# Block-wise products in the three merges of the triangular inverse

## The reference, cut to what matters

```
a = where(strict, einsum('bhnid,bhnjd->bhnij', k_beta, k) * decay, 0.0)
rhs = concatenate([v * beta, k_beta * exp(cum)])
sol = triangular_solve(a + eye, rhs, lower=True, unit_diagonal=True)
```

## Time and profile before

| | |
|---|---|
| median of 3 runs | 2837.27 us (2835.69 to 2837.76) |
| profiled execution | 2833.87 us |
| its span, first to last instruction | 2832.0 us |
| mean granted TensorE clock | 0.930 |
| PE / DVE / ACT / POOL busy | 91% / 51% / 28% / 7% |
| passes at L938, L948, L927 | 480, 480, 160 |

### The profile page before, as it was taken

The page is one execution under the profiler, slowest core; times in us unless marked ns, Lnnn a source line. Parts: engine busy times, 40 slices in busy tenths (PEclk is TensorE's granted clock), DMA queues, the critical chain, the costliest instruction groups (busy, mean ns, idle before and its releaser), DMA issues.

```text
span 2832.0 us, 39867 instructions
## 1 busy us (share of the span) xinstructions
PE 2587.9 (91%) x16152; PEld 2269.9 (80%) x16152; DVE 1454.4 (51%) x2004; ACT 801.6 (28%) x1031; POOL 204.1 (7%) x166
## 2 busy tenths in 40 slices
PE   6998888868899999998998899999898778999998
PEld 6997888857799999998987688887685444688886
DVE  5776555655345344453364567667414555434433
ACT  5322222212422212231222322223222354323222
POOL 1000101011000000010000100002001200100001
PEclk9997999989699999999976999999898889899998
DMA  3222222231122222222200254444221000122221
GB/s 125 87 75 71 78 78 74 59 86 31 76 78 88 90 90 89 89 99 81 76 13 0 89 178 165 152 158 163 97 74 45 0 0 0 61 103 89 96 97 60
DMA packets 91921, 230.90 MB, mean 82 GB/s; under 512 B 59946, under 2 KB 61564, under 8 KB 67620
## 3 DMA queue, kind: packets, MB, share of 16 engines
q1 hardware_dynamic: 86272, 197.04, 21.6%
q10 hardware_dynamic: 5540, 32.30, 3.3%
HBM read 217.67 MB, written 11.64 MB: 81 GB/s over the span
## 4 chain that ended last, share of the span: by engine, by line
PE 78%; DVE 11%; DMA 4%; ACT 3%; issue 2%; POOL 0%; DVEq 0%; SPq 0%; ACTq 0%; POOLq 0%
PE ps L285 60%; DMA g_D<-scr_g 2%; PE ps L449 2%; PE ps L475 1%; PE ps L948 1%; PE ps L938 1%; PE ps L289 1%; DVE wlo L308 1%; PE ps L2122 1%; PE ps L2104 1%; DVE g_tmp L1082 1%; PE ps L1571 1%; PE ps L1572 1%; PE ps L955 1%; DVE a_mx L2188 1%
## 5 line engine op out<-in xcount | busy, mean ns | idle before, releaser
L285 PE MATMUL ps<-xa_hi,whi 128*128 128x264 f32 (+1 forms) x2512 | 656.4, 320 | 44.0 <-DVE wlo L308 19.8
L285 PE MATMUL ps<-xa_lo,whi 128*128 128x264 f32 (+1 forms) x2512 | 652.1, 319 | 0.0
L285 PE MATMUL ps<-xa_hi,wlo 128*128 128x264 f32 (+1 forms) x2512 | 649.8, 318 | 0.0
L308 DVE TENSOR_TENSOR wlo<-raw,whi 128x2048 fp32r<-128x2048 f32 x161 | 373.5, 2320 | 261.2 <-ACT whi L301 261.2
L285 PEld LDWEIGHTS ps<-xa_hi,whi 128*128 128x128 f32 x2512 | 419.2, 191 | 86.6 <-issue 33.2
L301 ACT ACTIVATE whi<-raw 128x2048 fp32r<-128x2048 f32 x161 | 307.5, 1910 | 598.0 <-PE ps L285 581.1
L285 PEld LDWEIGHTS ps<-xa_lo,whi 128*128 128x128 f32 x2512 | 419.4, 191 | 29.7
L285 PEld LDWEIGHTS ps<-xa_hi,wlo 128*128 128x128 f32 x2512 | 418.6, 191 | 30.3
L285 PE MATMUL ps<-xb_hi,whi 128*128 128x264 f32 (+1 forms) x1280 | 384.0, 340 | 9.9 <-DVE xb_lo L1688 8.1
L285 PE MATMUL ps<-xb_lo,whi 128*128 128x264 f32 (+1 forms) x1280 | 385.1, 341 | 0.0
L285 PE MATMUL ps<-xb_hi,wlo 128*128 128x264 f32 (+1 forms) x1280 | 383.6, 340 | 0.0
(11 more groups left out here) (386 smaller groups left out, 2919.8 us busy)
## 6 DMA issues: line engine op xcount, KB each, us to landing
raw<-weights SPq DMA_DIRECT2D x161, 1024.0 KB, 4.9
mod_w<-weights_mod ACTq DMA_DIRECT2D x24, 1024.0 KB, 4.8
g_EC<-scr_g SPq DMA_DIRECT2D x10, 424.0 KB, 4.8
scr_z<-z_st SPq DMA_DIRECT2D x16, 264.0 KB, 2.4
g_D<-scr_g SPq DMA_DIRECT2D x10, 371.0 KB, 6.2
scr_a<-g_AT SPq DMA_DIRECT2D x10, 318.0 KB
h<-x_in ACTq DMA_DIRECT2D x4, 528.0 KB, 8.2
z_a<-scr_z SPq DMA_DIRECT2D x1, 2112.0 KB, 12.4
```

Of the source, the lines that this page charges most:

```text
L285: mm = pe.matmul(ps[:, at_ + step * c + bank, 0:tn], w[:, hb.slot, k, c * P:(c + 1) * P], x[:, k, t0:t0 + tn], start=(k == 0 and n == 0), ...
L308: dve.tensor_tensor(wlo[:, hb.slot], raw[:, hb.raw_slot], whi[:, hb.slot].bitcast(F32), ALU.subtract).then_inc(S("w_lo"), 1)
```

## The change

The products of a merge are cut to the blocks that it needs. A new function lists them: three pairs in merge 0 (32x32 tiles at 0, 32, 64, of which the products use 16 columns), two in merge 1 (32 wide, the second with 10 rows), one in merge 2 (64 by 42). The transposes become products with the identity on the same tiles. As some columns of the PSUM banks are then never written by these products, DVE clears columns 264 to 511 of banks 0 to 2 and 4 to 6 at the head of the stage, in place of a mere increment of the semaphore `z_ev`, and PE waits for both before its first product.

```diff
--- before.py
+++ after.py
@@ -846,6 +846,14 @@
 
             return slice(t // 2 * CH, t // 2 * CH + CH)
 
+        def tiles_of_merge(l):
+
+            if l == 0:
+                return [(slice(a, a + 2 * BLK), slice(a, a + 2 * BLK), a, a + BLK, BLK, BLK) for a in range(0, 6 * BLK, 2 * BLK)]
+            n = 2 * BLK * l
+            return [(slice(a, a + n), slice(a + n, min(CH, a + 2 * n)), a, a + n, n, min(CH, a + 2 * n) - a - n) for a in range(0, CH, 2 * n)
+                    if a + n < CH]
+
         def groups_of(t):
 
             return [(x, 2 * (t % 2) + x) for x in range(2)]
@@ -924,7 +932,8 @@
                             if l == 1 and z < N_Z:
                                 pe.wait_ge(S("z_ev"), 2 + nth(z, x))
                             for q in range(4):
-                                mm = pe.transpose(ps[0:CH, 4 * x + 1, q * CH:(q + 1) * CH], g_U[0:CH, 4 * x + q, 0:CH], ident[0:CH, 0:CH])
+                                for a, _, i, _, n, _ in tiles_of_merge(l):
+                                    mm = pe.matmul(ps[a, 4 * x + 1, q * CH + i:q * CH + i + n], g_U[a, 4 * x + q, a], ident[a, a], start=True, stop=True)
                             mm.then_inc(S("g_uT"), 1)
                     for x, g in groups_of(t):
                         if l:
@@ -935,8 +944,9 @@
                             if t < HALVES - 1:
                                 pe.wait_ge(S("g_A"), nth(t + 1, x))
                         for q in range(4):
-                            mm = pe.matmul(ps[0:CH, 4 * x, q * CH:(q + 1) * CH], g_AT[t % 2][0:CH, 4 * x + q, :], g_TV[0:CH, 4 * x + q, 0:CH],
-                                           start=True, stop=True)
+                            for a, b, i, _, n, _ in tiles_of_merge(l):
+                                mm = pe.matmul(ps[b, 4 * x, q * CH + i:q * CH + i + n], g_AT[t % 2][a, 4 * x + q, b], g_TV[a, 4 * x + q, i:i + n],
+                                               start=True, stop=True)
                         mm.then_inc(S("g_P"), 1)
                     for x, g in groups_of(t):
                         pe.wait_ge(S("g_Pc"), 2 * MERGES * t + 2 * l + x + 1)
@@ -945,8 +955,9 @@
                             if z < N_Z:
                                 pe.wait_ge(S("z_ev"), 2 + nth(z, x))
                         for q in range(4):
-                            mm = pe.matmul(ps[0:CH, 4 * x + 2, q * CH:(q + 1) * CH], g_B1[0:CH, 4 * x + q, :], g_U[0:CH, 4 * x + q, 0:CH],
-                                           start=True, stop=True)
+                            for a, b, i, j, n, m in tiles_of_merge(l):
+                                mm = pe.matmul(ps[i:i + n, 4 * x + 2, q * CH + j:q * CH + j + m], g_B1[b, 4 * x + q, i:i + n], g_U[b, 4 * x + q, j:j + m],
+                                               start=True, stop=True)
                         mm.then_inc(S("g_XU"), 1)
                 for x, g in groups_of(t):
                     pe.wait_ge(S("g_r"), nth(t, x))
@@ -970,6 +981,7 @@
                                        start=True, stop=True)
                     mm.then_inc(S("g_inc"), 1)
 
+            pe.wait_ge(S("z_ev"), 2)
             kk(0)
             for n in range(Z_EARLY):
                 z_block(n)
@@ -1149,7 +1161,8 @@
                 if z < N_Z:
                     dve_split(dve, HalfBlock(HB_GDN_OUT + z + 2))
 
-            dve.sem_inc(S("z_ev"), 2)
+            for x in range(2):
+                dve.memset(ps[:, 4 * x:4 * x + 3, 2 * P + 8:4 * P], 0.0).then_inc(S("z_ev"), 1)
             dve.wait_ge(S("in"), IN_FIRST + 32)
             differences(0)
             matrices(0)
```

## The result

The changed kernel takes 2845.82 us, the median of 8 runs (2841.41 to 2848.49), against 2835.90 us for the kernel before, also 8 runs (2832.46 to 2837.82). The ratio is 1.0035, with a 95% interval of 1.0024 to 1.0045: +9.9 us, slower. The forecast was 2861, +23.6. The profiled execution of the changed kernel took 2848.49 us (span 2846.6), 14.6 us more than the profiled one of before (2833.87), so the two traces have somewhat more to explain than the medians do.

The account below looks back on a forecast made before the run. PE and the merges' PE-ACT-DVE ring were taken to bind almost equally. Steps +15.8, low-clock excess -13.5 and +1.6 give +3.9; with clock +18 and clearing +1.7, +23.6 us: 2857 profiled, median 2861, range 2820 to 2893.

Parts of the forecast that it names:

- rival (d): Small passes step at 53 ns and the clock stays as now: +5.6 us, 2843; chance 0.18.
- I take the middle, 53 ns: Step between PE passes up to 32 wide in the merges, taken between 31 and 76 ns.
- +15.8: Merges over ten halves at full clock: us added by 2400 passes instead of 1120, at 53 or 58 ns each.
- the lower bound: PE step scaled down with operand width: 31 ns for 32 wide, 58 ns for 64 wide.
- rival (b): Merge tiles on different rows and columns run side by side: ring -18.4, excess -8, clearing +1.7; -25 us, 2812; chance 0.10.
- Small passes hardly feel the clock: Merges at the lower clock: a small pass takes 58 ns against 53 at full clock.
- the ring: Each merge's cycle: PE transpose, ACT copy, PE product P, ACT copy, PE product XU, DVE predicated copy; 4.52 us in merge 1.
- low-clock excess: Extra time of merge 0 and 1 groups running at the lower clock before; expected to go, -13.5 us.
- +1.6: Merges: us left at the lower clock, some 300 small passes at 5 ns each.
- nothing to give, as said: Merge 2 gains nothing in nine halves, as DVE's small inverses for the next half cover it; -0.45 us in the last.
- The clock term: Clock still low at L955 behind the merges: 3.6 instead of 1.79 us per half, +18 us; ends 0 and about +35.
- The clearing: Two PSUM memsets at the stage head delay the first product: +1.7 us on the chain, between +0.5 and +2.3.

Follow-up runs that it names:

- Experiment 4: Kernel before with the PSUM clearing and only merge 2 cut to its 64 by 42 tile: 2861.61 us, ratio 1.0099.
- experiment 3: Kernel before with the PSUM clearing and merges 0 and 1 in tiles, merge 2 over the full 106: 2837.20 us, ratio 1.0008.
- experiments 8: Kernel before, no tiles or clearing, with unused wide products (10, 24 and 4) filling PE's large idle gaps: 2828.24 us, ratio 0.9992.
- 10: Changed kernel with PE's large gaps and the handovers in every merge filled by unused products of dense data: 2874.84 us, ratio 1.0146.
- experiment 1: Kernel before with only the two PSUM memsets and PE's wait for them: 2834.43 us, ratio 0.9999.
- experiments 2: Kernel before with the PSUM clearing and only merge 0 in 32x32 tiles: 2842.82 us, ratio 1.0031.
- experiment 12: Kernel before with the PSUM clearing, only merge 0 tiled, and PE's large gaps filled by unused products of dense data: 2842.83 us, ratio 1.0026.
- experiments 5: Changed kernel with unused wide products filling PE's large idle gaps around merge 0: 2840.82 us, ratio 1.0030.
- 13: Kernel before with the clearing; in merge 2 alone P and XU use 64 and 42 rows, all 106 columns: 2847.64 us, ratio 1.0050.

## Why the prediction was right or wrong, step by step

**Direction and mechanism held, the size didn't.** Slower by over 0.2% had the largest chance. The time lies in the range, but 15 us under the forecast, and nearest to rival (d), which gets its 2843 from a clock that stays as it was: right number, wrong reason.

**The failed step is "I take the middle, 53 ns", the term of the sum that gave +15.8.** The step is 10.7 ns on three tiles, about 15 ns on two ((0.33 - 0.11) / 15 at 706.03). It has two parts. On one tile a pass of 32 columns takes 32 ns and one of 64 columns 58 ns: that is the lower bound which I had carried down in proportion to the width (31 and 58 ns), and the reason to go above it, "two instructions for each pass must cost something that doesn't shrink", was wrong. And the tiles run beside each other, rival (b)'s mechanism, to which I gave 0.10. The earlier trace rows were the wrong neighbour for that: they load 88 columns on all 128 rows. "Small passes hardly feel the clock" fell too: the same 48 passes at granted clock 0.50 take 1.05 us (t = 8), a step of about 19 ns.

**Rival (b)'s gain came only in part.** It had -18 for the ring and -8 of excess, and the merges give -14.3. By half: the four z halves t = 0, 1, 3, 4 give -14.5, the other six together +0.3. Cut at the predicated copies of x = 0, us before and after:

| halves | first P to copy of merge 0 | from there to copy of merge 1 | from there to L955 / L966 |
|---|---|---|---|
| t = 0 to 5 | 29.0, 32.8 | 40.2, 23.3 | 36.7, 36.1 |
| t = 6 to 8 | 13.6, 7.0 | 14.0, 19.7 | 17.9, 18.0 |
| t = 9 | 3.8, 4.0 | 4.5, 3.7 | 5.3, 6.0 |

In the z halves the gain is in the middle column. Its lines in t = 1, DVE of the kernel before and of the changed one:

```profile
373.27 0.62 DVE L1135 COPY_PREDICATED g_U<-g_maskU,ps 106x424 f32<-106x424 uint32 x1
...
380.58 0.65 DVE L1135 COPY_PREDICATED g_U<-g_maskU,ps 106x424 f32<-106x424 uint32 x1 [2.50 <-PE ps L948]
```

```profile
375.64 1.32 DVE L1147 COPY_PREDICATED g_U<-g_maskU,ps 106x424 f32<-106x424 uint32 x2
...
379.53 1.33 DVE L1147 COPY_PREDICATED g_U<-g_maskU,ps 106x424 f32<-106x424 uint32 x2 [0.40 <-PE ps L959]
```

From copy to copy of x = 0 it was 7.31 us, with XU of merge 0 and T and P of merge 1 at the lower clock, and is 3.89, of which DVE is busy for all but 0.40. At full clock the kernel before needs 4.89 (t = 5). So of the -16.9 us in six halves some 6 are the shorter groups, as (b) had them, and 10.9 the low-clock excess, for which the -13.5 over the whole stage was too small. The terms of the steps, +15.8 and +1.6, have no counterpart at all.

What hid the rest was not the step. In the z halves the first copy still waits for the store behind the z block, and the longer waits, in t = 2 and 5 above all, take 3.8 us back. In t = 9 merge 0 waits for DVE (2.97 us at 706.03), and merge 2 costs 0.7 us more: at the low clock its P takes 1.71 us, more than the wide one's 1.57. In the other nine halves merge 2 has nothing to give, as said. And in t = 6 to 8 merge 0 gives 6.6 us and a new wait takes 5.7 of them back, as in t = 8 of the changed kernel, DVE:

```profile
674.27 1.15 DVE L1147 COPY_PREDICATED g_U<-g_maskU,ps 106x424 f32<-106x424 uint32 x2
678.51 0.17 DVE L1066 COPY g_X<-ones 56x16 f32<-56x16 f32 x1 [3.09 <-DMA g_X<-scr_a]
...
680.71 1.13 DVE L1147 COPY_PREDICATED g_U<-g_maskU,ps 106x424 f32<-106x424 uint32 x2
```

The small inverses of the next half now wait 3.09 us for the transfer that lays out their input (2.32 and 4.26 us in t = 6 and 7), and merge 1's copy stands behind them in DVE's order. From the first P to L966 it is 14.77 us, where 14.81 stood before. I had named the order of the DVE, and not that its input comes by DMA.

**The clock term was right in kind and low in size:** +18 forecast, +23.0 measured, inside its ends of 0 and 35. L966 gives 17.3 (3.7 instead of 1.97 us in all ten halves), as counted; I put nothing for the groups behind it, and they give 5.7. Experiment 4 has the same price with merge 2's tile alone, and experiment 3 has none of it without that tile; the way there differs, for in experiment 4 the clock falls behind merge 2, and in the changed kernel it is low from merge 1 on. The sentence that by the page alone the term would be 0, "since PE has no more gaps than before", had its premise wrong: the shorter groups leave longer ones, 2.97 us before T of merge 1 in t = 9, where it was 1.37. That busy records alone don't hold the clock, as read from the earlier trace rows, held in 709.70 to 715.00 and in experiments 8 and 10.

**The clearing** was +1.7 and is +1.8 in the trace; experiment 1 finds no cost in the time.

With the measured sizes the prediction's own sum is -14.3 + 23.0 + 1.8 = +10.5, against +9.9 by the medians. (Experiment 1, with the passes of before, has 168.6 us of merges where the profiled run of before has 165.0, so each of these sums is good to some 4 us, and that the last one fits so closely is luck.)

**What stays open.** Why merge 0 alone (experiments 2 and 12) costs 7 to 9 us in the median: in the profile of 12, which is near its median, the merges take 5.7 us more than in that of before and 2.1 more than in that of experiment 1, less than the spread of some 4 us lets one read; why the same stream is granted 0.50 once and 1.00 another time (experiments 5 and 8; t = 1 and 4 of 13); and which part of experiment 4's fall is due to the narrow passes and which to the longer gap behind them. No version tried beats the kernel before beyond its interval.

## What to carry to other kernels

Cutting products to the blocks that they need pays only where PE's passes are on the chain and nothing dense follows soon: look first for what covers the ring (another engine's order, a store, a transfer) and at the granted clock of the next dense group, for a few narrow passes can cost that group twice its time. Leave the last group before dense work as wide as it is where something else covers it, as DVE covered merge 2 here. A filler pass belongs into measured idle time only, and its effect on the clock has to be seen in the windows, not assumed.

## What was unexpected of the hardware

- On one tile a pass of 32 columns takes 32 ns; three tiles beside each other share that, 10.7 ns for each pass. 64 columns take 58 ns (64 or 106 rows), 106 columns 93 ns (42, 64 or 106 rows).
- 5.3 us of 64-wide passes with PE busy for 5.26 of them stay at 0.50, and 9.95 us of passes over 128 rows and 128 columns get 0.52 in one run, where another run gives the same 48 passes 1.00 and 5.51 us.
- The clock can fall without idle time: with merge 0 tiled and its wait filled, the wide group behind it took 2.88 us (experiment 12, t = 9), where it took 1.57 in the kernel before.
- A memset of 128x744 in PSUM takes 0.73 us.
